# The finishing step of an expert loop: own rows by a second gather instead of a scaled copy

## What is computed

```python
def moe(x, w_router, w_gate, w_up, w_down):
    ...
    h = jax.nn.silu(jnp.einsum('nd,edf->nef', xt, w_gate)) * jnp.einsum('nd,edf->nef', xt, w_up)
    y = jnp.einsum('nef,efd->nd', h * gate.astype(h.dtype)[..., None], w_down)
    return y.reshape(shp)

def post_block(x, mixed, w_out, ln_g, ln_b, w_router, w_gate, w_up, w_down):
    x = layer_norm(DEEPNORM_ALPHA * x + mixed @ w_out, ln_g[0], ln_b[0])
    return layer_norm(DEEPNORM_ALPHA * x + moe(x, w_router, w_gate, w_up, w_down), ln_g[1], ln_b[1])
```

## Time and profile before

| what | us |
|---|---|
| runs without a profile | 1209.68, 1220.87, 1221.68 (median 1220.87) |
| the profiled execution | 1215.53 |
| its span, first to last instruction | 1213.8 |
| busy: TensorE matmuls | 1117.2 (92%) |
| busy: VectorE | 495.0 (41%) |
| busy: ScalarE | 418.0 (34%) |
| busy: POOL | 145.0 (12%) |

### The profile page before, as it was taken

One profiled execution on the slowest core, in us unless ns is written; L12 is line 12 of the kernel. 1 busy time (PEld: TensorE's weight loads), 2 busy tenths in 40 slices (PEclk: granted clock), 3 DMA queues, 4 the chain that ended last, 5 costly groups with the idle time before them and its releaser, 6 DMA issues.

```text
span 1213.8 us, 14858 instructions
## 1 busy us (share of the span) xinstructions
PE 1117.2 (92%) x4726; PEld 599.8 (49%) x4727; DVE 495.0 (41%) x1010; ACT 418.0 (34%) x766; POOL 145.0 (12%) x198
## 2 busy tenths in 40 slices
PE   7999999999999979999998899996589999999990
PEld 6646755444555434446455445554544444444440
DVE  2112333346543551441335222226513656565664
ACT  0101333457212145353332111011023655655654
POOL 4100000000000010000000000000012434343442
PEclk9999999999999879999999899997589999999996
DMA  8312331532110041114705441114075669787831
GB/s 235 102 36 104 106 139 70 184 123 53 70 70 1 3 74 52 34 46 10 202 7 164 186 156 70 52 61 165 18 260 195 237 240 370 284 287 260 301 96 65
DMA packets 117851, 157.39 MB, mean 130 GB/s; under 512 B 30346, under 2 KB 89034, under 8 KB 117770
## 3 DMA queue, kind: packets, MB, share of 16 engines
q1 hardware_dynamic: 90474, 103.98, 27.5%
q10 hardware_dynamic: 16416, 30.17, 6.8%
q0 software_dynamic: 10912, 22.57, 5.6%
HBM read 138.94 MB, written 52.73 MB: 158 GB/s over the span
## 4 chain that ended last, share of the span: by engine, by line
PE 74%; DMA 9%; DVE 6%; issue 4%; ACT 3%; SPq 3%; POOL 1%; ACTq 0%; POOLq 0%; DVEq 0%
PE psum_all L1437 19%; PE psum_all L1946 10%; PE psum_all L1553 8%; PE psum_all L2031 7%; DMA arena<-x_scratch,tok_now 5%; PE psum_all L1508 4%; PE psum_all L2019 4%; PE psum_all L1584 3%; PE psum_all L1618 3%; DMA arena<-slot_rows,partner_now 2%; PE psum_all L1642 2%; PE psum_all L2002 2%; PE psum_all L1610 1%; PE psum_all L1581 1%; PE psum_all L1906 1%
## 5 line engine op out<-in xcount | busy, mean ns | idle before, releaser
L1437 PE MATMUL psum_all<-arena 128*128 128x512 f32 (+7 forms) x800 | 232.4, 462 | 0.0
L2031 PE MATMUL psum_all<-arena 128*128 x400 | 178.6, 600 | 2.0 <-ACT arena L1341 2.0
L1437 PEld LDWEIGHTS psum_all<-arena 128*128 128x128 f32 (+1 forms) x800 | 129.4, 180 | 89.2 <-issue 63.2
L1946 PE MATMUL psum_all<-arena 128*128 128x512 f32 (+1 forms) x288 | 120.0, 599 | 0.0
L2031 PEld LDWEIGHTS psum_all<-arena 128*128 128x128 f32 x400 | 75.0, 193 | 88.1 <-issue 88.1
L1107 ACT ACTIVATE psum_all<-psum_all,neg_max 128x128 f32<-128x128 f32 (+7 forms) x96 | 65.6, 684 | 136.6 <-DVE neg_max L2163 136.2
L1553 PE MATMUL psum_all<-arena 128*128 128x512 f32 (+1 forms) x288 | 100.7, 505 | 0.0
L2019 PE MATMUL psum_all<-arena 128*128 x200 | 92.6, 607 | 1.1 <-ACT arena L1384 1.1
L1946 PEld LDWEIGHTS psum_all<-arena 128*128 128x128 f32 (+1 forms) x288 | 50.9, 187 | 62.6 <-issue 62.5
L1553 PEld LDWEIGHTS psum_all<-arena 128*128 128x128 f32 x288 | 48.0, 196 | 49.3 <-issue 48.9
L1018 POOL COPY tok_now<-slot_tok 128x1 int32 (+1 forms) x26 | 10.4, 400 | 493.1 <-DVE slot_tok L2690 426.1
(11 more groups left out here) (406 smaller groups left out, 1473.2 us busy)
## 6 DMA issues: line engine op xcount, KB each, us to landing
slot_rows<-slot_rows ACTq DMA_DIRECT2D x8, 2048.0 KB, 8.8
arena<-in_w_exp_gate SPq DMA_DIRECT2D x16, 1024.0 KB, 9.4
arena<-in_w_exp_up SPq DMA_DIRECT2D x16, 1024.0 KB, 12.3
arena<-in_w_exp_down SPq DMA_DIRECT2D x16, 1024.0 KB, 14.3
slot_rows<-arena ACTq DMA_DIRECT2D x24, 512.0 KB, 6.1
arena<-in_x_prompt SPq DMA_DIRECT2D x16, 512.0 KB, 4.0
arena<-in_cache_fox_kv SPq DMA_DIRECT2D x32, 256.0 KB, 3.4
arena<-in_w_in SPq DMA_DIRECT2D x2, 2048.0 KB, 11.3
```

What stands on the lines that cost most here:

```text
L1437: ins = nc.tensor.matmul(row_bank(j)[p0:p0 + n, 0:cn], xT[:, k, tok0(t):tok0(t) + n], wv[:, k, c0:c0 + cn], start=(k == 0), stop=(k == KD ...
L1946: ins = nc.tensor.matmul(psum[2 * (t % 2) + i][p0:p0 + n, :], lhs, wo[:, k, i * 512:(i + 1) * 512], start=(k == 0), stop=(k == KD - 1), ti ...
L2031: ins = nc.tensor.matmul(psum[0][:], xT_slot[:, k, :], arena[:, bass.ds(w_at + k * 2 * F, 2 * F)], start=(k == 0), stop=(k == KD - 1))
```

## The change

ScalarE's scaled copy and its four buffers go. When a tile is finished, the tokens' own rows are gathered once more from `x1_scratch`, by the indices that the store uses (`row_of`), so for later slots only, and into one buffer, `own_rows`. POOL issues this gather right behind the partner gather. VectorE's first add becomes a fused multiply and add of own rows and partner rows into `sum_row`, which the square and the normalization read. POOL no longer waits for `ax_ready` ahead of an x gather. Some waits for `indices_ready`, long satisfied, move with the first use of the index tables, and `own_rows` is cleared once beside `partner_rows`.

```diff
@@ -506,15 +506,8 @@
         sil = at(R_X + 6 * D, F)
         h_row = at(R_X + 6 * D + F, F)
         h_T = at(R_X + 6 * D + 2 * F, F // P, P)
-        N_AX = 4
-        partner_rows = at(R_W + N_AX * D, D)
-        z_row, out_row, squares = [at(R_W + (N_AX + 1 + i) * D, D) for i in range(3)]
-
-        def scaled_x(t):
-
-            return arena[:, bass.ds((t % N_AX) * D + R_W, D)]
-
-        ax_ready = sem("ax_ready")
+        partner_rows, own_rows, sum_row, z_row, out_row, squares = [at(R_W + i * D, D) for i in range(6)]
+        own_now = sb("own_now", [P, 1], I32)
         partner_set = sem("partner_set")
         partner_in = sem("partner_in")
         partner_used = sem("partner_used")
@@ -542,6 +535,7 @@
         partner_now = sb("partner_now", [P, 1], I32)
         row_now = sb("row_now", [P, 1], I32)
         row_set = sem("row_set")
+        own_in = sem("own_in")
         partner_cleared = sem("partner_cleared")
         xs_turned = sem("xs_turned")
         xs_dve = sem("xs_dve")
@@ -1024,18 +1018,24 @@
             def gather_partner(col, n, used):
 
                 stored = n * 16 if isinstance(n, int) else pool.to_reg(n * 16)
+                pool.wait_ge(indices_ready, 1)
                 if used is not None:
                     pool.wait_ge(partner_used, used)
-                pool.tensor_copy(partner_now[:], partner_of[:, col]).then_inc(partner_set, 1)
+                pool.tensor_copy(partner_now[:], partner_of[:, col])
+                pool.tensor_copy(own_now[:], row_of[:, col]).then_inc(partner_set, 1)
                 pool.wait_ge(indices_ready, 1)
                 pool.wait_ge(ys_stored, stored)
                 pool.wait_ge(partner_set, n)
                 pool.indirect_dma_start(partner_rows[:], None, slot_rows,
                                         bass.IndirectOffsetOnAxis(ap=partner_now[:], axis=0),
                                         bounds_check=last_slot, oob_is_err=False).then_inc(partner_in, 16)
+                pool.indirect_dma_start(own_rows[:], None, x1_dram,
+                                        bass.IndirectOffsetOnAxis(ap=own_now[:], axis=0),
+                                        bounds_check=last_token, oob_is_err=False).then_inc(own_in, 16)
 
             def store_finished(col, n):
 
+                pool.wait_ge(indices_ready, 1)
                 pool.wait_ge(out_ready, n)
                 pool.tensor_copy(row_now[:], row_of[:, col]).then_inc(row_set, 1)
                 pool.wait_ge(indices_ready, 1)
@@ -1052,7 +1052,6 @@
             def next_x(t):
 
                 pool.wait_ge(xs_turned, t * 2 + 2)
-                pool.wait_ge(ax_ready, t + 1)
                 gather_x1(bass.ds(t + 1, 1), t + 2 if isinstance(t, int) else pool.to_reg(t + 2))
 
             last_slot, last_token = pool.to_reg(NSL * P - 1), pool.to_reg(TOK - 1)
@@ -1062,7 +1061,8 @@
             next_x(2)
             pool.wait_ge(indices_ready, 1)
             pool.memset(partner_rows[:], 0.0).then_inc(partner_cleared, 1)
-            pool.wait_ge(partner_cleared, 1)
+            pool.memset(own_rows[:], 0.0).then_inc(partner_cleared, 1)
+            pool.wait_ge(partner_cleared, 2)
             next_x(3)
             gather_partner(slice(1, 2), 1, None)
             with pool.Fori(1, last - 2) as n:
@@ -1340,13 +1340,6 @@
                 act.wait_ge(xs_turned, n_turned)
                 nc.scalar.copy(xT_slot[:, 4:8, :], psum[5][:].rearrange("p (k n) -> p k n", k=4)).then_inc(xs_act, 1)
 
-            def scale_x(t, freed):
-
-                act.wait_ge(xs_in, t * 16 + 16)
-                if freed is not None:
-                    act.wait_ge(z_done, freed)
-                nc.scalar.activation(scaled_x(t), x_slot[:], ACT.Copy, scale=ALPHA).then_inc(ax_ready, 1)
-
             def copy_rows(n):
 
                 if not isinstance(n, int) or n > 0:
@@ -1361,19 +1354,18 @@
 
             def square(t):
 
-                nc.scalar.activation(squares[:], scaled_x(t), ACT.Square, bias=fin_s[:, 1:2],
+                nc.scalar.activation(squares[:], sum_row[:], ACT.Square, bias=fin_s[:, 1:2],
                                      accum_out=fin_s[:, 2:3]).then_inc(fin_squared, 1)
                 act.wait_ge(fin_squared, t)
                 nc.scalar.activation(fin_s[:, 2:3], fin_s[:, 2:3], ACT.Sqrt, bias=lnc[:, 0:1], scale=1.0 / D
                                      ).then_inc(fin_std, 1)
                 nc.scalar.activation(fin_s[:, 4:5], lnc[:, 0:1], ACT.Silu)
 
-            def slot_tile(t, before, finish, freed):
+            def slot_tile(t, before, finish):
 
                 act.wait_ge(hid_done, t + 1)
                 nc.scalar.activation(sil[:], psum[0][:, 0:F], ACT.Silu).then_inc(sil_ready, 1)
                 copy_x(t * 2 + 4)
-                scale_x(t + 1, freed)
                 some = before is not None
                 done = finish is not None
                 if done:
@@ -1390,15 +1382,14 @@
             act.wait_ge(slots_ready, 1)
             last = last_tile(act)
             copy_x(2)
-            scale_x(0, None)
-            slot_tile(0, None, None, None)
+            slot_tile(0, None, None)
             act.wait_ge(slots_cleared, 16 * len(CLEAR_AFTER))
             for t in range(1, 3):
-                slot_tile(t, t - 1, None, None)
-            slot_tile(3, 2, 1, None)
+                slot_tile(t, t - 1, None)
+            slot_tile(3, 2, 1)
             before = last_tile(act, 1)
             with act.Fori(1, last_tile(act, 2)) as m:
-                slot_tile(m + 3, m + 2, m + 1, m)
+                slot_tile(m + 3, m + 2, m + 1)
             act.wait_ge(fin_mean, before)
             copy_rows(last)
             square(before)
@@ -2718,10 +2709,11 @@
 
             def add_rows(t):
 
-                A = scaled_x(t)
+                A = sum_row[:]
                 dve.wait_ge(partner_in, t * 16)
-                dve.wait_ge(ax_ready, t + 1)
-                V.tensor_tensor(A, A, partner_rows[:], ALU.add).then_inc(partner_used, 1)
+                dve.wait_ge(own_in, t * 16)
+                V.scalar_tensor_tensor(out=A, in0=own_rows[:], scalar=ALPHA, in1=partner_rows[:], op0=ALU.mult, op1=ALU.add
+                                       ).then_inc(partner_used, 1)
                 dve.wait_ge(y_act, t + 1)
                 dve.wait_ge(y_dve, t + 1)
                 dve.wait_ge(partner_used, t)
@@ -2733,7 +2725,7 @@
             def normalize(t, before):
 
                 dve.wait_ge(fin_mean, t)
-                V.scalar_tensor_tensor(out=z_row[:], in0=scaled_x(t), scalar=fin_s[:, 1:2], in1=ln_row[1][:, 0, :],
+                V.scalar_tensor_tensor(out=z_row[:], in0=sum_row[:], scalar=fin_s[:, 1:2], in1=ln_row[1][:, 0, :],
                                        op0=ALU.add, op1=ALU.mult).then_inc(z_done, 1)
                 dve.wait_ge(fin_std, t)
                 V.reciprocal(fin_s[:, 3:4], fin_s[:, 2:3]).then_inc(fin_rstd, 1)
```

## The result

The changed kernel is **slower**: 1233.82 us in the median of 6 runs (1228.12 to 1242.09), beside 1219.7 for the kernel before; ratio 1.0127 [1.0089, 1.0165]. In a second series it was 1.0085 [1.0052, 1.0118]. The forecast was 1215 with a range of 1205 to 1228. The profiled execution took 1232.44 us, its span 1230.7.

What follows compares the result with a forecast made beforehand. TensorE was taken as the bound, losing only 11.35 us in the loop; terms -1.8 - 1.8 - 0.8 + 1.5 + 0.1 + 1.7 - 0.1 = -1.2 us, set against the runs' mean of 1216.9, gave about 1215 us, range 1205 to 1228.

Steps and rivals of the forecast that it cites:

- the second gather: Expert loop: late own rows make the 0.85 us stall grow to about 2.3, +1.5 us (bounds +1.0 and +1.9).
- The sentence on the held copy: POOL, each tile: VectorE can block the added index copy; where it does, the late own gather costs 0.9 us more.
- Rival C: Expert loop: the five-engine loop of gather, add, store and next gathers closes more tightly, +12.9 us, 1230 us; chance 0.17.
- D + 17.5 us: Time between own issues two tiles apart, D being the gather's landing (9.3 us under weights, 5.5 without); two tiles give 22.8.
- The freed x gather: Tiles 0 and 1 and loop: earlier x gathers shorten TensorE's waits, by -1.8, -1.8, -0.8 and -0.1 us.
- The waits at the start: First two tiles: TensorE's waits of 0.38 and 1.41 us go, -1.8 us (bound 0 if streaming weights keep the gather late).
- The 1.34 us stall: Expert loop, the one stall where ScalarE was the last releaser: it goes, -1.8 us (bounds -1.0 and -1.8).
- B: Expert loop: the x gather is freed everywhere and all stalls go, -11.4 us, 1205 us; chance 0.16.
- The tail: After the last matmul: the second issue and landing move the add by 1.1 to 2.3 us, finishes in series, +1.7 us.
- The scaled copy's removal: ScalarE: 27.6 us of copies turn into waiting for the mean; nothing gained but the earlier x gather.
- The fused add: VectorE: 1.28 us in place of 1.22, hidden behind TensorE's tiles but for +0.1 us at the end.
- D: Expert loop, as a rival: the gathered bytes push TensorE wherever DMA is busy, +8 us, 1225 us; chance 0.14.

Runs made afterwards that it cites:

- e1: The changed kernel without the second gather and without the add's wait for it; both index copies stay; ratio to the kernel before 0.9958 [0.9926, 0.9990].
- e3: The changed kernel with one POOL copy fetching both partner and own indices from one table; ratio to the kernel before 1.0037 [1.0010, 1.0063].
- e2: The changed kernel with the own gather still issued and awaited, but its rows skipped by a bounds check of 0; ratio to the kernel before 0.9992 [0.9963, 1.0020].
- e5: The kernel before, with ScalarE's scaled copy moved ahead of its copy of the turned x, right behind the silu; ratio to the kernel before 0.9963 [0.9933, 0.9993].

## Why the prediction was wrong

**The step that failed is the second gather**, put at +1.5 us in the loop. Measured against e1 it is about +16 (3.0 to 18.9). Two things went into it.

*Its issue.* The text put the own gather 1.08 us behind the partner gather. Even unheld it is 1.34 in e3 (a gap of 0.30 us stands between the two issues); in the change it is 2.3 in 14 of 24 tiles, 1.9 in the mean. The Trainium skill (SBUF — State Buffer, "Who interferes with whom") was cited for VectorE's two-input operations and GpSimd instructions that read SBUF, and applied to the index copy alone. The DMA's issue reads its indices from SBUF too, and the traces show it held by just such operations. The sentence on the held copy (0.9 us more) had the size, at the wrong instruction, and no term of the sum has it, where 14 of 24 issues are held. The trace before had shown the hold, at the x gather's issue: 14 of its 25 take 1.36 to 1.82 us there, the other 11 0.96 to 1.16.

```profile
952.37 1.23 DVE L2724 TENSOR_TENSOR arena<-arena 128x1024 f32 x1 [1.65 <-DMA arena<-slot_rows,partner_now]
...
952.64 1.82 POOL L1021 DMA_INDIRECT arena<-x_scratch,tok_now  x1 [0.78 <-POOL tok_now L1018]
```

*Its place.* The term was charged to one stall. Rival C had the account that decides: the loop closes in D + 17.5 us and slips where D is over 5.3. In the tile shown D is 8.1, and the loop takes 25.8. The prediction gave C 0.17 because "a tile without streaming weights resets the loop". That happens: of 22 tiles four lose over 2 us (6.3, 5.5, 2.4 and 2.1), the others less than that or nothing. It was not enough. C's 1230 us lies 4 below the median, in part by luck: it has 13.0 us of loop where the own gather costs 16, counts no gain of the freed x gather in the loop, where e1 shows 6.5 against before's mean, and has 1.7 of tail where 5.1 are measured.

**The freed x gather** was worth more than forecast: -1.8 - 1.8 - 0.8 - 0.1 = -4.5; e1 has -8.6 to -10.1 from tile 0 to the end by the traces, -5.1 by the times. The waits at the start went (-1.3), but the 1.40 us for weights took part of it back; the bound of 0 had thought of the weights, as what would keep the gather late. The 1.34 us stall did not go in the changed kernel: it is 1.71 (at 1105.55), the same tile. In e1 it is gone, but in the second trace of before too, so one trace does not show what ended it. Without the second gather most of B's stalls go, not all: e1 keeps 3.0 us in the loop and the 1.40.

**The tail**, +1.7, came to +5.1 (mean). POOL and VectorE in the first trace:

```profile
1193.57 2.06 POOL L1029 DMA_INDIRECT arena<-slot_rows,partner_now  x1 [0.83 <-POOL own_now L1025]
1195.93 0.99 POOL L1032 DMA_INDIRECT arena<-x_scratch,own_now  x1 [0.31 <-issue]
...
1204.73 2.04 POOL L1029 DMA_INDIRECT arena<-slot_rows,partner_now  x1 [0.83 <-POOL own_now L1025]
1207.08 0.99 POOL L1032 DMA_INDIRECT arena<-x_scratch,own_now  x1 [0.31 <-issue]
...
1218.98 1.00 POOL L1043 DMA_INDIRECT out<-arena,row_now  x1 [0.83 <-POOL row_now L1040]
```

```profile
1201.15 1.23 DVE L2715 SCALAR_TENSOR_TENSOR arena<-arena 128x1024 f32<-128x1024 f32 x1 [2.54 <-DMA arena<-x_scratch,own_now]
...
1210.53 1.23 DVE L2715 SCALAR_TENSOR_TENSOR arena<-arena 128x1024 f32<-128x1024 f32 x1 [1.45 <-DMA arena<-x_scratch,own_now]
```

Counted from tile 24's start (1181.39, and 1169.98 before), the add at 1201.15 is 2.1 us later than that of the earlier trace rows, inside the bounds of 1.1 to 2.3, but not by the step that gave them. The add at 1187.60 waited for no gather: its 0.17 us end in "issue", and VectorE came straight from L2744 of the tile before (1186.14, 1.28 us). So its 5.5 us from the issue are no landing, and the 5.5 of the prediction, for the tail and for D without weights, is only an upper bound of one. The next add is not: its gather waits for this add, is held again (2.04 us), and the last add comes 3.7 us later, the last store 3.5. The text let the second finish run in series on VectorE; it waits for its own rows. The other 2.0 us no step had: from the last store's issue to the end is 9.75 us before and 11.71 after (below).

For the landing, the Trainium skill (DMA: Bandwidth & Descriptors, "Anatomy of one DMA") gave an estimate of 3.2 us. Counted to the add that waits for it, the last own gather takes 3.45 (1207.08 to 1210.53), close to the estimate, the one before 5.2, and the one at 948.91, while weights stream, 8.1.

**What held.** The scaled copy's removal gave ScalarE nothing but waiting: 27.6 us of copies less, 28.1 more for the mean. The fused add cost nothing that shows. The x gather waits for the transposes, its 18 waits for ScalarE are gone. D did not come as it was put: TensorE waits once for weights, 1.4 us. But e2 shows that the bytes matter, by a later landing. And of its own list of signs, the one for C came true: the add's waits more than doubled (11.8 to 27.5), and TensorE's stalls grew with them.

**The trace as a base.** Eleven microseconds of stalls were booked to tenths, tile by tile; the same kernel's second trace lost 7.6 us, with the largest loss in another tile. Only sums over the loop, and the tail, bear such terms, and before's loop bears them only to 4 us. A small slip besides: the mean of 1216.9 less 1.2 is 1215.7, not 1215.

## What to carry to other kernels

Where a finishing chain and a prefetch share one in-order queue, cost an added transfer by the loop that it closes: sum it from issue to issue, compare with the period of the engine that bounds, and give the rival that it makes its due when the sum is over. Before an instruction is added ahead of a DMA issue, look at what the neighbouring engine is in the middle of 0.2 us later. Here the buffer was freed more cheaply by moving its reader forward in its engine's order (e5, one line) than by fetching the same rows twice.

## What the runs showed of the hardware that was not expected

**An indirect DMA's issue on GpSimd is held by a VectorE operation with two inputs in SBUF** (128x1024, 1.2 to 1.3 us) that it finds under way, until about 0.9 us after that operation's end. In the twelve traces, no issue that begins 0.07 us into one or less is held (0.99 to 1.04 us for partner and own gathers), and every one that begins 0.08 us in or later ends 0.85 to 0.94 us behind it: begun 0.12 to 0.18 us in, it takes 2.00 to 2.07 us; 0.7 us in, 1.4. VectorE's copies out of PSUM (L2708) do not hold it.

**Skipped rows still make packets.** The pages' lines on queue 0 (packets, MB, share), before, after and in e2:

```profile
q0 software_dynamic: 10912, 22.57, 5.6%
...
q0 software_dynamic: 14368, 27.04, 6.7%
...
q0 software_dynamic: 14368, 22.59, 5.7%
```

The 24 own gathers add 3456 packets, 144 each, whether 1088 rows move (after, +4.47 MB in the queue) or one (e2, +0.02). By the sizes in the traces, 16 of the 144 are packets of 4 bytes, and each skipped row is another of 4 bytes. In the queue's share of time they hardly show (5.7% beside 5.6%).

**The end of the program has a fixed part.** From the start of the last store's issue to the end of the span are 9.75 us in each of the six traces without the second gather, and 11.71 in each of the six with it, moved rows or none. Which step of the program's end that is, the traces do not show.
